# Neighbourhood attention in blocks of 8x16 queries and 12x32 keys, two heads as two 64-row tiles, relative bias from masked tables in DRAM

## The reference

```
# q, k, v: 1024 tokens = 16 rows x 64 columns, 8 heads of 64
rs        = clip(r - 4, 0, 16 - 8)            # first of 8 key rows of query row r
col_start = clip(col - 8, 0, 64 - 16)         # first of 16 key columns of a query column
s = q . k[rs:rs+8, col_start:col_start+16] * 64**-0.5 + rpb[head, key_row - r + 7, key_col - col + 15]
out = softmax(s over the 8 x 16 keys) @ v[the same keys]
```

## Time and profile before

| | |
|---|---|
| median of 3 runs | 1843.69 us (1843.58 to 1845.81) |
| the profiled execution, its own time | 1837.65 us |
| its span in the profile | 1835.9 us |
| PE busy | 1629.6 us, 89% of the span |
| DVE, ACT, POOL busy | 724.1, 510.9, 509.0 us |
| the attention's pairs | from about 275 to 579 us of the span |

### The profile page before, as it was taken

The page is one execution under the profiler, slowest core; times in us unless marked ns, Lnnn a source line. Parts: engine busy times, 40 slices in busy tenths (PEclk is TensorE's granted clock), DMA queues, the critical chain, the costliest instruction groups (busy, mean ns, idle before and its releaser), DMA issues.

```text
span 1835.9 us, 37277 instructions
## 1 busy us (share of the span) xinstructions
PE 1629.6 (89%) x14820; PEld 1179.3 (64%) x14820; DVE 724.1 (39%) x1319; ACT 510.9 (28%) x902; POOL 509.0 (28%) x472
## 2 busy tenths in 40 slices
PE   2799999999998999999998994399999989999960
PEld 1677786777766787787886883155555555555630
DVE  1745536565656334435223756011111111111118
ACT  1456534444455112111002210022222222222214
POOL 4522221111113332333331210432333323232332
PEclk8899999999999999999999995699999999999985
DMA  9541010101001433443122316579999999979836
GB/s 311 164 141 33 24 46 24 35 24 30 17 12 41 124 99 97 126 143 98 51 80 105 100 40 266 206 274 399 400 400 401 400 400 402 400 300 397 327 116 223
DMA packets 178855, 333.88 MB, mean 182 GB/s; under 512 B 38382, under 2 KB 100470, under 8 KB 178750
## 3 DMA queue, kind: packets, MB, share of 16 engines
q1 hardware_dynamic: 145774, 272.59, 40.2%
q0 software_dynamic: 24256, 42.96, 7.0%
q10 hardware_dynamic: 8720, 16.80, 3.0%
HBM read 302.44 MB, written 29.72 MB: 181 GB/s over the span
## 4 chain that ended last, share of the span: by engine, by line
PE 55%; DVE 7%; DMA 3%; issue 2%; POOL 1%; ACT 0%; DVEq 0%; SPq 0%; ACTq 0%; POOLq 0%
PE ps L950 18%; PE ps L711 13%; PE ps L961 9%; PE ps L879 7%; PE ps L904 5%; PE ps L940 1%; DMA w_exp<-in_w_exp_up 1%; DVE act L1613 1%; PE ps L911 1%; POOL d_list L614 1%; DVE br_lo L1440 1%; DMA ada_g<-in_ada_w 1%; DVE res L1646 1%; DVE y L1636 1%; DVE x L1637 1%
## 5 line engine op out<-in xcount | busy, mean ns | idle before, releaser
L950 PE MATMUL ps<-w_exp,xT 128*32 128x256 f32 x6272 | 350.9, 382 | 4.5 <-DMA w_exp<-in_w_exp_up 4.5
L711 PE MATMUL ps<-u_hi,w_hi 128*128 128x512 f32 x768 | 312.6, 407 | 0.9 <-ACT lx L1035 0.9
L711 PE MATMUL ps<-u_lo,w_hi 128*128 128x512 f32 x768 | 305.7, 398 | 0.0
L711 PE MATMUL ps<-u_hi,w_lo 128*128 128x512 f32 x768 | 300.8, 392 | 0.0
L950 PEld LDWEIGHTS ps<-w_exp,xT 128*32 128x32 f32 x6272 | 208.0, 111 | 138.6 <-issue 8.6
L541 POOL CAST w_hi<-w_raw 128x1024 fp32r<-128x1024 f32 x48 | 60.8, 1267 | 571.2 <-issue 335.0
L961 PE MATMUL ps<-w_exp,actT 128*32 128x256 f32 x3136 | 179.5, 381 | 0.0
L1613 DVE TENSOR_TENSOR act<-act,ps 64x256 f32<-64x256 f32 x98 | 41.6, 424 | 342.6 <-ACT act L1203 341.1
L711 PEld LDWEIGHTS ps<-u_hi,w_hi 128*128 128x128 f32 x768 | 145.1, 189 | 36.2 <-issue 9.4
L711 PEld LDWEIGHTS ps<-u_hi,w_lo 128*128 128x128 f32 x768 | 144.9, 189 | 28.6
L711 PEld LDWEIGHTS ps<-u_lo,w_hi 128*128 128x128 f32 x768 | 145.3, 189 | 25.1 <-issue 1.0
(11 more groups left out here) (254 smaller groups left out, 2277.9 us busy)
## 6 DMA issues: line engine op xcount, KB each, us to landing
w_exp<-in_w_exp_gate SPq DMA_DIRECT2D x32, 2048.0 KB, 27.0
w_exp<-in_w_exp_up SPq DMA_DIRECT2D x32, 2048.0 KB, 26.6
w_exp<-in_w_exp_down SPq DMA_DIRECT2D x32, 2048.0 KB, 27.0
ada_g<-in_ada_w ACTq DMA_DIRECT2D x32, 512.0 KB, 3.8
d_y<-yb POOLq DMA_DIRECT2D x98, 128.0 KB, 7.3
w_raw<-in_w_in SPq DMA_DIRECT2D x24, 512.0 KB, 4.1
w_raw<-in_w_branch_gate SPq DMA_DIRECT2D x24, 512.0 KB, 4.1
ada<-in_ada_w SPq DMA_DIRECT2D x4, 2048.0 KB, 15.0
```

The lines of the kernel that those rows point to most:

```text
L711: ins = pe.matmul(ps[:, 5 + h, :], a[par][:, kc, :], b[:, kc, HF[h]], start=(n == 1), stop=(n == MM))
L950: last = pe.matmul(ps[CAP * n:CAP * (n + 1), 2 + h, 0:QT], x, w[n // 2][:, off:off + QT], start=(kc == 0), stop=(kc == KC - 1))
```

## The change

Units become blocks. A unit is 8 query rows x 16 columns = 128 queries of both heads, with 12 key rows x 32 key columns = 384 keys for each head: 8 units per pair, 32 in all. The two heads are no longer put on a block diagonal. Each head's scores are a matmul over its own 64 partitions, 128 queries against 384 keys (two matmuls of a unit, in two PSUM banks). `stage_q`, `q_bd`, `o_bd` and the transpose of `o_bd` go. DVE now scales the probabilities themselves by the reciprocal sum (128x384, once per head), six transposes follow, and the product with V has the values of a head (64 columns) as the stationary operand and `probT` as the moving one, so that the output lies in 64 partitions per head, features first, as `y_na` wants it; ACT copies it in one instruction.

The fill stays 144 matmuls of 128x512 per pair, 18 per unit, 9 ahead of the product with V and 9 behind. V is laid out by ACT in four overlapping column blocks of 32 (two instructions per half instead of one). K is projected ahead of Q. The last job ahead of the pairs is cut: after 6 matmuls of its second half come the last V transposes and the first scores, then its other 18.

The bias: POOL builds shifted and column-masked tables once (`build_table`, 2 x 3 instructions of 92x512), SP stores them to DRAM in 8 DMAs of 128-byte runs, and loads a tile of 2 x 128x384 for each of 6 sets per pair (24 sets, 48 DMAs of 192 KB, 1536-byte runs, in place of 8 of 240 KB), into a ring of three; POOL adds a row mask to each (128x768, 24 times, in place of 128x960, 4 times). SP may load a set when the set three before it has been read.

```diff
+QR, QC = 8, 16
+KR, KW = 12, 32
+KEYS = KR * KW
+KT = KEYS // P
+UNITS = ROWS // QR * CBLK
+COL0 = (0, 8, 24, 32)
...
+            def scores(u):
+                hp, half, c = place(u)
+                if c == 0:
+                    pe.wait_ge(job_evac, 2 * (PRO + PER * hp) - 1 + half)
+                pe.wait_ge(s_biased, 2 * u)
+                for h in range(2):
+                    own = slice(DH * h, DH * (h + 1))
+                    keys = cells(kT[own, hp % 2])[:, 4 * half:4 * half + KR, COL0[c]:COL0[c] + KW]
+                    pe.matmul(ps[:, SBANK[h], 0:KEYS], qT[own, hp % 2, half, c, :], keys, start=True, stop=True).then_inc(s_ps, 1)
...
-            pe.wait_ge(job_evac, 2 * PRO)
-            scores(0, 0, 0)
...
+            last_job = job_half_mms(PRO - 1, (PRO - 1) % 2, 1, PRO, 2 * (PRO - 1))
+            run(last_job, MM // 4)
+            pe.wait_ge(vt_evac, 3)
+            transpose_v(3)
+            scores(0)
+            run(last_job)
...
+                for r in range(UNITS):
+                    u = hp * UNITS + r
+                    _, half, c = place(u)
+                    if u + 1 < PAIRS * UNITS:
+                        scores(u + 1)
+                    pe.wait_ge(pt_ready, 2 * u)
+                    for h in range(2):
+                        pe.wait_ge(p_ready, 2 * u + h + 1)
+                        for i in range(KT):
+                            last = pe.transpose(ps[:, TBANK[h], i * P:(i + 1) * P], prob[:, u % 2, h, i * P:(i + 1) * P], ident[:])
+                        last.then_inc(pt_ps, 1)
+                    run(fg, SHARE // 2)
+                    pe.wait_ge(pt_ready, 2 * u + 2)
+                    if u >= 2:
+                        pe.wait_ge(y_ready, u - 1)
+                    cols = slice(u % 2 * P, (u % 2 + 1) * P)
+                    for i in range(KT):
+                        for h in range(2):
+                            own = slice(DH * h, DH * (h + 1))
+                            last = pe.matmul(ps[own, YBANK, cols], vtok[:, hp % 2, (half + i) * CBLK + c, own], probT[:, h, i, :],
+                                             start=(i == 0), stop=(i == KT - 1))
                     last.then_inc(o_ps, 1)
-                    run(fg, share - share // 2)
-
-                    pe.wait_ge(o_ready, done(u))
-                    pe.wait_ge(y_ready, done(u - 1))
-                    pe.transpose(ps[:, 4, 0:P], o_bd[r % 2][:], ident[:]).then_inc(ot_ps, 1)
+                    run(fg, SHARE - SHARE // 2)
...
+            def softmax(u):
+                dve.wait_ge(bias_ready, bias_set(u) + 1)
+                if u >= 2:
+                    dve.wait_ge(pt_ps, 2 * (u - 1))
+                sl = u % 2
+                for h in range(2):
+                    dve.wait_ge(s_ps, 2 * u + h + 1)
+                    ch.mark(dve.tensor_tensor(prob[:, sl, h, :], ps[:, SBANK[h], 0:KEYS], bias[:, bias_set(u) % 3, h, :], ADD))
+                ch.sync()
+                for h in range(2):
+                    dve.tensor_reduce(nmax[:, sl, h:h + 1], prob[:, sl, h, :], AX.X, ALU.max, negate=True).then_inc(s_biased, 1)
+                for h in range(2):
+                    dve.wait_ge(p_exp, 2 * u + h + 1)
+                    ch(dve.reciprocal(rinv[:, sl, h:h + 1], rsum[:, sl, h:h + 1]))
+                    dve.tensor_scalar(prob[:, sl, h, :], prob[:, sl, h, :], rinv[:, sl, h:h + 1], None, MUL).then_inc(p_ready, 1)
...
+            def load_bias(n):
+                if n >= 3:
+                    sp.wait_ge(s_biased, 2 * (last_unit(n - 3) + 1))
+                hp, half, kind = n // SETS, n // KINDS % 2, n % KINDS
                 for side in range(2):
+                    first = (((2 * hp + side) * KINDS + kind) * QC * PADR + 4 * (1 - half)) * KW
+                    src = bass.AP(d_table, first, [[KW, QR], [PADR * KW, QC], [1, KEYS]])
+                    sp.dma_start(bias[:, n % 3, side, :], src).then_inc(ld_bias[n % 3], 16)
```

More of the change, by code:

```diff
@@ L135, in build @@
         w_lo = [at(f"w_lo{i}", 187 + 4 * i, [P, KC, P], f32r) for i in range(2)]
[L136 to L140, removed]
+        rpb_pad = at("rpb_pad", 204, [4 * PADR, 2, PADC])
+        table = at("table", 100, [4 * PADR, KINDS * QC, KW])
+        colmask = at("colmask", 106, [4 * PADR, KINDS * QC, KW])
         t_cos = at("t_cos", 128, [P, TT // 2, HALF])
@@ L555, in _, with build_table, mask_bias @@
                 pool.tensor_tensor(u_lo[:, kc, HF[th]], u_full[n % 4][:], u_hi[:, kc, HF[th]].bitcast(f32), SUB).then_inc(u_lo_odd, 1)
[L557 to L562, removed]
+            def build_table(g):
+                if g:
+                    pool.wait_ge(st_table, 16 * 4)
+                for kind in range(KINDS):
+                    v = rpb_pad[:, g, QC - 8 * kind:QC - 8 * kind + KW]
+                    shifted = bass.AP(v.tensor, v.offset, [v.ap[0], [1, QC], [1, KW]])
+                    own = slice(kind * QC, (kind + 1) * QC)
+                    ins = pool.tensor_tensor(table[:, own, :], shifted, colmask[:, own, :], ADD)
+                    if kind == KINDS - 1:
+                        ins.then_inc(table_set, 1)
+                    else:
+                        ch.mark(ins)
+            def mask_bias(n):
+                pool.wait_ge(ld_bias[n % 3], 32 * (n // 3 + 1))
+                b3 = bias[:, n % 3].rearrange("p h (r c) -> p (h r) c", c=KW)
+                rows = rowmask[:, n // KINDS % 2, :].unsqueeze(2).to_broadcast([P, 2 * KR, KW])
+                pool.tensor_tensor(b3, b3, rows, ADD).then_inc(bias_ready, 1)
             pool.wait_ge(ld_const, 16 * 5)
             split(2, 0, 32, 2)
-            mask_bias(0, 32)
+            pool.wait_ge(rpb_in, 16 * HEADS)
+            pool.wait_ge(ld_mask, 16)
+            build_table(0)
             pool.wait_ge(zero_set, 1)
@@ L1418, in pair @@
+            softmax(0)
+            for hp in range(PAIRS):
+                for r in range(UNITS):
+                    u = hp * UNITS + r
+                    if u + 1 < PAIRS * UNITS:
+                        softmax(u + 1)
                     if hp < PAIRS - 1 and VT0 <= r < VT0 + 4:
@@ L1420, in pair @@
                         dve.wait_ge(vt_ps, hp * 4 + (g + 5))
-                        v_tiles(g, nxt)
-            for hp in range(PAIRS):
-                pair(hp)
+                        v_tiles(g, (hp + 1) % 2)
             yr = lx[:, 1, BC - 1, :]
@@ L1655, in constants @@
 def constants():
-    w, cc = np.arange(GRID_W)[:, None], np.arange(GRID_W)[None, :]
-    start = np.clip(w - WIN_C // 2, 0, GRID_W - WIN_C)
-    window = np.where((cc >= start) & (cc < start + WIN_C), 0.0, NEG)
+    i, key = QC - 1 - np.arange(QC)[:, None], np.arange(KW)[None, :]
+    first = [np.maximum(i - WIN_C // 2, 0), i, np.minimum(i + WIN_C // 2, KW - WIN_C)]
+    colmask = np.stack([np.where((key >= f0) & (key < f0 + WIN_C), 0.0, NEG) for f0 in first])
+    r, row = QR - 1 - np.arange(P)[:, None] // QC, np.arange(KR)[None, :]
+    first = [np.maximum(r - WIN_R // 2, 0), np.minimum(r, WIN_R // 2)]
+    rowmask = np.stack([np.tile(np.where((row >= f0) & (row < f0 + WIN_R), 0.0, NEG), (1, 2)) for f0 in first], 1)
     j = np.arange(P)
```

325 lines of the change are left out of this document (155 added, 170 removed).

## The result

The changed kernel takes 1821.23 us (median of 4 runs, 1817.78 to 1822.62), the kernel before 1843.63 us in the same comparison (4 runs, 1843.43 to 1845.81): a ratio of 0.9873 with a 95% interval of 0.9856 to 0.989. It is 22.4 us faster, where 83.4 were forecast, and lies outside the range of 1746 to 1794. The profiled execution took 1822.62 us, its span is 1820.8.

A forecast was written before the change was run, and what follows sets the result against it. PE, in order and busy 288.66 of 294 us in the attention, was taken as the bound. Gains of 77.1 (units), 5 (waits) and 1.3 (start) sum to 83.4 us, from 1843.69 to 1760.3, said as 1760; range 1746 to 1794.

The forecast's parts named there:

- the part on the bias: Bias tables, stores and set loads: sets come in time, stores take some 43 us unseen; cost 0, at worst a few us.
- PE's unit: Attention pairs: a new unit takes 6.43 us of PE against 8.84 for two old ones; 77.1 us less in 32 units.
- Scores, product and changes of shape: Per attention unit on PE: 0.65 for scores, 0.65 for the product with V, 0.28 us for four tile shape changes.
- Transposes: Per attention unit on PE: six at 0.09 each, 0.53 us; the transpose of `o_bd` gone.
- fills: Per attention unit on PE: 18 at about 0.23 each plus two restarts at 0.09 more, 4.32 us.
- change of shape: PE switching tile shape, four times per attention unit: 0.07 us each, between 0 and 0.13.
- The start: From the last job's end into the first attention units: 6.8 us lost becomes 5.5, a gain of 1.3, between 0 and 4.
- The waits: PE's idle time and lower clock in the attention pairs: 3 us after, a gain of 5, between 0 and 10.
- rival 4: Bias ring in the attention pairs holds units up, kernel slower than before; 34 us per set would give 1852; chance 0.03.
- The sum: Whole kernel: 77.1 from units, 5 from waits, 1.3 from the start, 83.4 us faster in all.
- the part on the port: DVE scalings in the attention: 0.33 us, 2 or more where POOL runs, with 2.5 us to spare ahead of PE.

The follow-up runs named there:

- 25 rows: Changed kernel with 25 rows per head in the bias tables in place of 23, the rest padding; 1768.73 us (1 run).
- 24 rows: Changed kernel with 24 rows per head in the bias tables in place of 23, one of padding; 1769.19 us, again on another chip 1763.53 us.
- early exp: Kernel with 24 rows, ACT copies the last half of Q behind the first unit's exps instead of ahead; 1754.39 us (4 runs).
- 29 rows: Changed kernel with 29 rows per head in the bias tables in place of 23, the rest padding; 1849.61 us (1 run).

## Why the prediction was wrong

- **The step that failed** is the last of the part on the bias: "SP's job loads behind them have a job's time of slack. Cost 0, at worst a few us." That part took the stores at the rate of a bias load of before, which has 960 runs in 4.7 us, and got 43 us. The stores held SP for 61.8 and 38.2 us. That load has 128 rows, the store has 23, and the rate of one doesn't carry over to the other. The slack was not worked out either: the sum was checked against the tables' first use and not against the weights queued behind four stores in a row, and POOL's own wait for the first stores, with a split behind it, was not named at all. Whether 21 us for each four would have been hidden is not shown; with 25 rows 32.1 us for the first four were. Cost: 51.5 us by the profile, 52 and 47.8 by the two comparisons with 24 rows.
- **PE's unit** was right in mechanism: 6.81 us for 6.43. Scores, product and changes of shape were 1.58 together and measured 1.66. Transposes were 0.53 and took 0.63, fills 4.32 and took 4.52: 0.38 us in all, 12 us over 32 units. What was priced too low is mostly the change of shape. Each run of nine fills has its first fill at 0.32 to 0.33 us, as the restarts had it, but also its last at 0.33 (385.12 - 384.79) and 0.31 (388.19 - 387.88). The last unit has no scores ahead of its transposes. There the last fill of the run takes 0.23 us and the six transposes 0.58 in place of 0.63:

```profile
548.87 0.39 PE L789 MATMUL ps<-u_hi,w_lo 128*128 128x512 f32 x1
549.10 0.82 PE L917 MATMUL ps<-ident,prob 128*128 128x128 f32 x6
549.68 0.48 PE L789 MATMUL ps<-u_hi,w_hi 128*128 128x512 f32 x1
```

  So 0.20 of the fills, 0.05 of the transposes and 0.08 of the rest belong to the changes of shape: about 0.61 us a unit in place of 0.28, or 0.15 each, above the 0.13 that the prediction had as its end.
- **The start** was to gain 1.3 us. The first product's unit lost 6.6 us to waits and low clock (13.45 from 272.12 to the next scores at 285.57 with 24 rows, less 6.81), about as much as before (6.8): waits of 3.1 and 0.6 us, and fills behind them at a granted clock that had fallen to 0.50. The cause was the one named, ACT's copy ahead of the first exp, as the early exp showed.
- **The waits** behaved: from 380 to 540 us PE is busy 159.37 of 160 us, and `bias_ready` ended none of DVE's waits. The ring of three (rival 4) never showed; POOL waited 89.0 us for bias loads, all of it under other work. From the last job's end to the merge's first job the profile was to show about 221 us; it shows 554.92 - 325.19 = 229.7. Of these 32 units of 6.81 are 217.9, and 11.8 are left where the prediction had 15.
- **The sum.** With the stores cured, the gain was 74.1 and 74.4 us in the two groups, for 83.4 forecast: 12 for the unit and 1 for the start are missing, a few us of it made up by waits that went as well. That the sum came near was thus in part luck. 1763.53 and 1769.19 us lie inside the range.

The scaling behaved as the part on the port had it, at other sizes: 0.42 us alone for 0.33, and 1.38 for the "2 us or more" where it meets a mask. The timelines of DVE and POOL in the changed kernel show one that starts ahead of a mask and one that meets it:

```profile
391.83 0.42 DVE L1475 TENSOR_SCALAR prob<-prob,rinv 128x384 f32<-128x384 f32 x1
...
392.43 1.38 DVE L1475 TENSOR_SCALAR prob<-prob,rinv 128x384 f32<-128x384 f32 x1
...
391.91 1.68 POOL L623 TENSOR_TENSOR bias<-bias,rowmask 128x768 f32<-128x768 f32 x1
```

The second ends 0.22 us behind the mask (393.81 and 393.59), and PE did not wait for it.

## What to carry to other kernels

Price a DMA by its own access pattern: its runs, and how many engines its outer size lets them share. Then price the queue that issues it: what is behind it, and how soon that is wanted. A store that nobody needs for 50 us can still stop the kernel, and one row of padding can be worth more than half of a large change.

## What was not expected of the hardware

- A DMA of 1104 runs of 128 bytes over 23 rows holds SP 12.9 us, of 1152 runs over 24 rows 0.72 us at the median. The stores move at 11 GB/s with 23 or 29 rows, at 55 with 25 and at 146 with 24.
- 23 runs of 6144 bytes move at 26 GB/s and hold SP for 0.65 us.
- Two score tiles of 64 rows in one array, and two product tiles of 64 columns, cost 0.64 to 0.65 us less per step than the same work in turns. A step of two is 0.85 and 0.81 us from start to start, and the 128x512 matmul ahead of it takes 0.08 to 0.10 us more.
- The expert step of the kernel with 24 rows was 12.27 us on one chip and 12.00 us on another, where the kernel before took 1843 and 1838 us. On a third, other kernels made from it had 12.00 us too.
